# Dense fp32r matmuls that take the columns of two halves of the tokens in turn, 8 at a time

## What is computed

```python
h = rmsnorm(x, norm_mix);  z = h @ w_in              # 2048 -> 16,464 columns
o_a, o_b, o_c = sparse_attention(z), block_attention(z), retention(z)
m = sig(g_a) * (o_a @ w_pa) + sig(g_b) * (o_b @ w_pb) + sig(g_c) * (o_c @ w_pc)
x = x + m @ w_out
h2 = rmsnorm(x, norm_ffn)
x = x + (gelu(conv3(h2 @ ffn_up)) * (h2 @ ffn_gate)) @ ffn_down
y = rmsnorm(x, norm_final)
```

## Time and profile before

| | |
|---|---|
| median of 3 runs | 2384.52 us (2384.14 to 2385.04) |
| the profiled execution, first to last instruction | 2383.5 us |
| what the median has beyond that span | 1.0 us |
| TensorE's granted clock over the span | 0.998 of 2.4 GHz |
| TensorE busy | 2351.6 us |
| VectorE busy | 1410.9 us |
| ScalarE busy | 919.1 us |
| bytes moved | 458.69 MB, 192 GB/s in the mean |

### The profile page before, as it was taken

How to read it: one execution, slowest core, us unless ns; L and a number is a source line. 1 busy time by engine, 2 the same in 40 slices (tenths; PEclk the granted TensorE clock), 3 DMA queues, 4 the chain that set the end, 5 groups by cost and what they waited for, 6 DMA issues and landing times.

```text
span 2383.5 us, 44504 instructions
## 1 busy us (share of the span) xinstructions
PE 2351.6 (99%) x17202; PEld 2270.1 (95%) x17202; DVE 1410.9 (59%) x2095; ACT 919.1 (39%) x1274; POOL 314.0 (13%) x629
## 2 busy tenths in 40 slices
PE   8999999999999999999999999999999999999997
PEld 8978999999999999998999999999999999999997
DVE  6535568989987545445456645666654356666443
ACT  5334444333333444334333344333333333333332
POOL 1135110000002322333200011000000000000001
PEclk9999999999999999999999999999999999999999
DMA  7448645546557988998776544444445544444553
GB/s 239 143 132 243 178 140 182 180 168 207 204 175 264 307 290 292 302 336 298 245 265 194 183 151 148 153 153 149 152 151 153 150 157 154 148 153 154 149 153 106
DMA packets 174434, 458.69 MB, mean 192 GB/s; under 512 B 25018, under 2 KB 74538, under 8 KB 174096
## 3 DMA queue, kind: packets, MB, share of 16 engines
q1 hardware_dynamic: 141040, 372.31, 47.9%
q0 software_dynamic: 26128, 75.67, 9.7%
q10 hardware_dynamic: 7056, 7.88, 0.9%
HBM read 425.27 MB, written 27.52 MB: 190 GB/s over the span
## 4 chain that ended last, share of the span: by engine, by line
PE 95%; DVE 2%; ACT 1%; issue 1%; DMA 0%; DVEq 0%; SPq 0%; ACTq 0%
PE ps L789 87%; PE ps L1061 1%; PE ps L1014 1%; PE ps L860 1%; PE ps L1044 1%; ACT w_hi L1102 1%; DMA xT<-in_x 0%; PE ps L984 0%; PE ps L976 0%; PE ps L872 0%; PE ps L927 0%; PE ps L963 0%; PE ps L967 0%; PE ps L824 0%; PE ps L902 0%
## 5 line engine op out<-in xcount | busy, mean ns | idle before, releaser
L1353 DVE TENSOR_TENSOR w_lo<-w_raw,w_hi 128x1024 fp32r<-128x1024 f32 (+1 forms) x622 | 749.4, 1207 | 778.3 <-ACT w_hi L1102 775.3
L789 PE MATMUL ps<-h_hi,w_hi 128*128 128x320 f32 x3696 | 1160.6, 314 | 11.7 <-DVE w_lo L1353 9.5
L789 PE MATMUL ps<-h_lo,w_hi 128*128 128x320 f32 x3696 | 1132.3, 306 | 0.0
L789 PE MATMUL ps<-h_hi,w_lo 128*128 128x320 f32 x3696 | 1125.8, 305 | 0.0
L1102 ACT ACTIVATE w_hi<-w_raw 128x1024 fp32r<-128x1024 f32 (+1 forms) x622 | 647.4, 1043 | 802.2 <-PE ps L789 790.5
L789 PEld LDWEIGHTS ps<-h_hi,w_hi 128*128 128x128 f32 x3696 | 694.7, 188 | 41.9 <-issue 38.9
L789 PEld LDWEIGHTS ps<-h_lo,w_hi 128*128 128x128 f32 x3696 | 694.9, 188 | 0.4
L789 PEld LDWEIGHTS ps<-h_hi,w_lo 128*128 128x128 f32 x3696 | 694.5, 188 | 0.0
L789 PE MATMUL ps<-y_hi,w_hi 128*128 128x320 f32 x688 | 213.5, 310 | 1.7 <-DVE yt L1425 1.7
L789 PE MATMUL ps<-y_lo,w_hi 128*128 128x320 f32 x688 | 210.5, 306 | 0.0
L789 PE MATMUL ps<-y_hi,w_lo 128*128 128x320 f32 x688 | 209.2, 304 | 0.0
(11 more groups left out here) (322 smaller groups left out, 2063.4 us busy)
## 6 DMA issues: line engine op xcount, KB each, us to landing
w_raw<-in_w_in SPq DMA_DIRECT2D x258, 512.0 KB, 5.0
w_raw<-in_ffn_up SPq DMA_DIRECT2D x86, 512.0 KB, 3.9
w_raw<-in_ffn_gate SPq DMA_DIRECT2D x86, 512.0 KB, 3.7
w_raw<-in_ffn_down SPq DMA_DIRECT2D x80, 448.0 KB, 3.4
kpg<-in_cache_b_k SPq DMA_DIRECT2D x128, 128.0 KB, 4.5
vpg<-in_cache_b_v POOLq DMA_DIRECT2D x128, 128.0 KB, 5.0
kpg<-in_cache_a_k SPq DMA_DIRECT2D x128, 128.0 KB, 4.8
vpg<-in_cache_a_v POOLq DMA_DIRECT2D x128, 128.0 KB, 4.9
```

The source lines that it names most:

```text
L789: mm = mmul(bank[q][:, 0:T], wp[:, s, cols], xp[:, x.k0 + k, :], start=(x.first and k == 0 and t == 0), stop=(x.last and k == x.nk - 1 and ...
L1353: tt(w_lo[:, s, 0:n], w_raw[:, s, 0:n], w_hi[:, s, 0:n].bitcast(F32), ALU.subtract).then_inc(w_lo_done, 1)
```

## The change

A constant GRAIN = 8 and a view `woven` are added, and both the moving operand and the output of the dense matmul go through it. The view splits 320 columns into two halves (j, 160 columns or 640 bytes apart), each half into 20 pieces (i) of 8 columns (e), and walks them as piece 0 of the first half, piece 0 of the second half, piece 1 of the first half, and so on. The output is walked in the same way, so each column lands in PSUM where it did before.

```diff
+GRAIN = 8
...
+        def woven(x):
+
+            return x.rearrange("p (j i e) -> p i j e", j=2, e=GRAIN)
+
...
                         for t, (wp, xp) in enumerate(((w_hi, xh), (w_hi, xl), (w_lo, xh))):
-                            mm = mmul(bank[q][:, 0:T], wp[:, s, cols], xp[:, x.k0 + k, :],
+                            mm = mmul(woven(bank[q][:, 0:T]), wp[:, s, cols], woven(xp[:, x.k0 + k, :]),
                                       start=(x.first and k == 0 and t == 0), stop=(x.last and k == x.nk - 1 and t == 2))
```

## The result

The changed kernel takes 2472.32 us (median of 4, 2471.63 to 2472.72) against 2384.78 us for the kernel before (4 runs, 2384.14 to 2386.21): a ratio of 1.0364, 95% interval 1.035 to 1.0379. It is slower by 88 us. That lies outside the range that was given (2350 to 2440), and the likeliest case, no measurable change, did not come. The ratios here leave out runs in a slower state: one of the ten of the writing alone (2907.02 us, granted clock 0.751) and two of the four with jumps of 256 bytes (2546.43 and 2547.61 us).

A forecast was written before the change was run, and what follows sets the result against it. TensorE's pace of dense matmuls was taken as the bound. Nothing removed and breaks at 0 gave 2383.5 + 0 = 2383.5 us for the profiled execution, 2384.5 us as median of the runs; 8 in 10 range 2350 to 2440.

The forecast's parts named there:

- the likeliest case: Whole kernel: no measurable change, 2384.5 us, with its own range 2380 to 2389; chance 0.54.
- The bound: Dense matmul, line 789: TensorE's pace there, 144.5 to 147.1 ns a matmul, sets the end; 2,127 us, 89% of the span.
- Nothing removed, nothing moved: 0 us: Whole kernel: same operands, matmul count, columns, weights, waits and PSUM layout, no DMA or queue touched; 0 us.
- The reading side at 0: Dense matmul's moving operand: breaks in the read cost 0, since lines 1032 and 905 both last 219 ns.
- The writing side at 0: Dense matmul's PSUM output: breaks cost 0, taken from the reading rows, as the trace had no broken write.
- The 137.5 ns for 320 columns and 7.0 ns of slack: Dense matmul's 144.5 ns: 320 columns at 0.43 ns take 137.5, leaving 7.0 for going to the next matmul.
- Rival (3): Dense matmuls: new order of places slows the pace by 2.6 ns, 34 us, 2418 us, carried to 2440; chance 0.20.
- Rival (1): Dense matmul's PSUM write: each break stops the stream for one column; 2631 us, or 2528 with slack; chance 0.10.
- rival (2): Dense matmuls: short runs move at half the pace, 137.5 ns more each, 2,020 us, 4404 us; chance 0.08.
- Rival (4): Dense matmuls: new order keeps TensorE's two reads apart, 2.6 ns less each, 38 us less, 2346 us; chance 0.08.

## Why the prediction was wrong, point by point

**The bound** was right. The dense matmul's pace set the end, nothing else moved, and 5.9 to 6.65 ns a matmul (3.6 in the stage of oa, ob and m) explain the time.

**Nothing removed, nothing moved: 0 us** was right as well; DVE and the small matmuls take what they took (1411.3 us busy against 1410.9).

**The reading side at 0** is the step that failed. I took it from line 1032 against line 905. In the changed kernel line 1032 (now 1038) still shows this, with 0.03 and 0.23 us from start to start:

```profile
1019.68 0.22 PE L1038 MATMUL ps<-m,ecur 128*128 128x128 bf16 x1
1019.71 0.39 PE L795 MATMUL ps<-h_hi,w_hi 128*128 128x320 f32 x1
1019.94 0.31 PE L795 MATMUL ps<-h_lo,w_hi 128*128 128x320 f32 x1
```

The row was true but answered another question. It reads the same 16 bytes sixteen times. I had written that it returns to one place where the change jumps, and still let it carry the value. What the runs showed in place of the 0 is 6.65 ns a matmul on the reading side alone (2472.44 us, against 2384.99 for the writing alone). A break as such has no price in runs of 4 columns or more, since 39 and 79 of them come with 24 and 33 us less than before; what costs is the order in which the places follow, which a read that never leaves its place can't show. Line 1014 has runs of 512 bytes and only three jumps a matmul.

**The writing side at 0** was right, and it was the side that I feared. The Trainium skill's sentence against it (PSUM — Partial Sum Buffer, Specifications (TRN2)), that any access that isn't contiguous slows matmuls significantly, disagrees with the runs: 433.3 ns a triple for writes in runs of 2 to 80 columns, as in one run. With its other statement (the Trainium skill, Advanced Engine Details and Errata, PSUM Cachelines), that every two consecutive elements should be contiguous, the runs agree as far as they go: runs of 1 were not measured.

**The 137.5 ns for 320 columns and 7.0 ns of slack** were mis-sized. 0.43 ns a column was taken from bf16. For the dense operand one run costs 0.442 ns in the mean from 256 to 512 columns, 141.5 ns for 320, and 3 ns are left; and one run is no floor, since another order takes 142.2 ns a matmul and, with the placing matched, 140.0.

**Rival (3)** named the mechanism, a pace that shifts with the order of places, and was sized by the 2.6 ns between two stages. It measured 6.65 ns; the top of 2440 was too low by 32 us. Its reason, two reads of TensorE that meet, is shown only in part: the place of the weights relative to the moving operand moves the pace, the number of their columns doesn't. Its sign, three steps that change unequally, came (6.7, 3.4 and 10.0 ns). Rival (1) fell with the writing alone (2384.99 us), rival (2) with the pace itself, 151.1 ns and not about 280. Rival (4), the same shift downwards, did not come with this order but with its neighbours: 24, 33 and 51 us.

**Open**: what in the memory makes one order quick and another slow (the spacing alone does not tell: 640 bytes, slow, and 128, quick, differ by a multiple of 256), whether the jump or the number of pieces counts, why placing acts between successive operands when one operand repeated shows none of it, and why the stage of oa, ob and m gained nothing from jumps of 128 when it gained from jumps of 64. Whether a bf16 operand behaves the same was not tried.

## What to carry to other kernels

When TensorE's pace is the bound, the order in which a matmul walks its moving operand is a knob: over the same 320 columns and the same result it was worth from -1.4% to +5.6% of a whole kernel, and -2.1% with the placing of the weights matched to it. A cheap way to read it is a series of some 70 matmuls behind the kernel for each order and placing, paced by starts over whole triples of the steady part; what they showed came true in the kernel in sign each time and in size to within about a third. And a row that is near a change in form is no bound if it holds still where the change moves: ask what the row can't show before letting it stand for 0.

## What the runs showed of the hardware that I had not expected

- PSUM can be written in runs of 2 columns at no cost (433.3 ns a triple, as in one run).
- One run is not the quickest read: 320 columns take 144.4 ns a matmul, against 142.2 with pieces 128 bytes apart.
- Reads in runs of 2 fp32r columns (8 bytes) cost 206 ns a matmul at 640 bytes and 271 to 333 ns at other jumps, against 144.4 in one run; runs of 4 (16 bytes) cost 142 to 167. The Trainium skill (SBUF — State Buffer, Specifications (TRN2)) has lines of 16 bytes that want at least two hits; the step between runs of 2 and of 4 fits lines of 16 bytes. But a run of 2 is two hits and was slow all the same, and the spread among runs of whole lines, 426.5 to 502.2 ns a triple, is not in it.
- Steady triples came mostly in steps of 6.67 ns: 420.0, 426.7, 433.3, 440.0, 446.7, 453.3, 460.0. 6.67 ns is the time of 16 columns at 2.4 GHz. Why is not known.
- Moving the weights or the low activations by 256 bytes changes nothing (433.4 and 433.3); moving the weights or the moving operand by 32 to 224 bytes changes a triple of one run by 2 to 11 ns.
- The pace goes by where the two lie relative to each other: the weights moved by 32, 64 and 128 bytes (435.6, 440.0, 444.0) match the moving operand moved by 224, 192 and 128 (435.5, 440.0, 444.0).
